# Attention of 160 tiles: TensorE's order per tile becomes scores, values of the tile two back, turning of the tile one back

## The reference

```python
s = jnp.einsum('bqhd,bqkhd->bhqk', qb, kg) * ATTN_SCALE
s = jnp.where(valid[:, None], s, -jnp.inf)
p = jax.nn.softmax(s, axis=-1)
o = jnp.einsum('bhqk,bqkhd->bqhd', p, vg)
```

```python
def gqa_attention(q, k, v):
    ...
        logits = jnp.einsum("bqhgd,bkhd->bhgqk", qb, k).astype(jnp.float32) * scale
        p = jax.nn.softmax(logits, axis=-1).astype(v.dtype)
        return jnp.einsum("bhgqk,bkhd->bqhgd", p, v)
```

## Time and profile before

| | |
|---|---|
| median of 3 runs | 3273.68 us (3270.32 to 3275.79) |
| span of the profiled execution, its only time | 3279.7 us |
| TensorE busy | 3142.8 us (96%) |
| VectorE, ScalarE, GpSimd busy | 47%, 40%, 34% |
| scores L1347, 2064 matmuls | 213.3 us |
| turning L1805, 1312 | 182.9 us |
| values L1820, 2624 | 178.6 us |

### The profile page before, as it was taken

The page is one execution under the profiler, slowest core; times in us unless marked ns, Lnnn a source line. Parts: engine busy times, 40 slices in busy tenths (PEclk is TensorE's granted clock), DMA queues, the critical chain, the costliest instruction groups (busy, mean ns, idle before and its releaser), DMA issues. The chain is left out here.

```text
span 3279.7 us, 50609 instructions
## 1 busy us (share of the span) xinstructions
PE 3142.8 (96%) x20584; PEld 2584.5 (79%) x20584; DVE 1545.7 (47%) x2748; ACT 1307.4 (40%) x2383; POOL 1121.1 (34%) x613
## 2 busy tenths in 40 slices
PE   9989999999989999999999999999999998799999
PEld 7757788888667888888887888887888877688787
DVE  5963343227853344242376410268333349843473
ACT  4352333223433333233466222267222248723463
POOL 4531444446324444434201222243224422125202
PEclk9998999999999999999999999999999999999999
DMA  4344222324452223222000112110112200013102
GB/s 163 114 171 171 84 97 97 100 88 134 144 199 90 96 97 111 97 84 82 27 2 21 58 58 65 54 48 15 53 64 87 87 20 1 12 53 111 39 2 78
DMA packets 80806, 259.92 MB, mean 79 GB/s; under 512 B 11968, under 2 KB 13376, under 8 KB 80576
## 3 DMA queue, kind: packets, MB, share of 16 engines
q1 hardware_dynamic: 80576, 256.69, 23.6%
HBM read 239.34 MB, written 2.10 MB: 74 GB/s over the span
## 5 line engine op out<-in xcount | busy, mean ns | idle before, releaser
L188 PE MATMUL ps<-hs,head 128*128 128x512 f32 (+1 forms) x4176 | 864.1, 364 | 18.8 <-DVE hs L1068 8.6
L188 PE MATMUL ps<-hs,WS 128*128 128x512 f32 (+1 forms) x4176 | 858.3, 363 | 6.0 <-POOL WS L169 5.9
L188 PEld LDWEIGHTS ps<-hs,head 128*128 128x128 f32 x4176 | 711.2, 189 | 160.4 <-issue 13.4
L188 PEld LDWEIGHTS ps<-hs,WS 128*128 128x128 f32 x4176 | 713.0, 189 | 134.4 <-POOL WS L169 8.3
L169 POOL TENSOR_TENSOR WS<-W,WS 128x1024 fp32r<-128x1024 f32 x168 | 407.0, 2423 | 645.2 <-ACT WS L161 645.2
L169 POOL TENSOR_TENSOR head<-W,head 128x1024 fp32r<-128x1024 f32 x165 | 400.6, 2428 | 624.6 <-ACT head L161 624.6
L161 ACT CAST WS<-W 128x1024 fp32r<-128x1024 f32 x168 | 176.1, 1048 | 339.7 <-PE ps L188 314.1
L1838 ACT ACTIVATE prob<-ps,low 128x768 f32<-128x768 f32 (+4 forms) x320 | 223.4, 700 | 180.1 <-DVE low L1910 177.7
L1910 DVE TENSOR_REDUCE low<-ps 128x1 f32<-128x768 f32 (+4 forms) x320 | 216.6, 702 | 93.5 <-PE ps L1347 89.1
L161 ACT CAST head<-W 128x1024 fp32r<-128x1024 f32 x165 | 172.7, 1047 | 199.4 <-PE ps L188 196.0
L1347 PE MATMUL ps<-kk,qq 64*128 64x256 f32 (+3 forms) x2064 | 213.3, 333 | 24.8 <-ACT prob L1574 14.7
(11 more groups left out here) (323 smaller groups left out, 3756.9 us busy)
## 6 DMA issues: line engine op xcount, KB each, us to landing
W<-in_stream_dram SPq DMA_DIRECT2D x433, 512.0 KB, 3.3
swap<-prj SPq DMA_DIRECT2D x168, 64.0 KB, 2.5
band<-in_bias_band_dram SPq DMA_DIRECT2D x8, 512.0 KB, 3.6
prj<-prj SPq DMA_DIRECT2D x64, 64.0 KB, 2.8
xT<-in_x_dram SPq DMA_DIRECT2D x4, 512.0 KB, 6.3
out_dram<-xT SPq DMA_DIRECT2D x8, 256.0 KB, 2.7
W<-in_stream_dram SPq DMA_DIRECT2D x1, 1536.0 KB, 10.8
xT<-in_ctx_dram SPq DMA_DIRECT2D x1, 1024.0 KB, 7.4
```

What stands on the lines that cost most here:

```text
L188: last = pe.matmul(out, a(i), b(j), start=start and n == 0, stop=stop and n == 2)
```

## The change

On TensorE, the block that turns tile x-1 is moved behind the block that multiplies the values of tile x-2. The waits of both blocks go with them, and their contents stay as they are. The side work's mix stays ahead of both, its products behind both. No other engine's program is changed.

```diff
@@ -1793,18 +1793,6 @@
                             keep_running(pe, M, 4, 7)
                     if side:
                         side.mix(pe, x)
-                    if 1 <= x <= X:
-                        y = x - 1
-                        for hd in range(2):
-                            pe.wait_ge(exped, 2 * y + hd + 1)
-                            if y:
-                                pe.wait_ge(turn_copied, act_copies(y - 1) + 1 if hd == 0 else act_copies(y))
-                                if dve_copies(y) and (hd or W.tail(y)):
-                                    pe.wait_ge(dve_turn_copied, dve_copies(y))
-                            for j, sc in enumerate(W.columns(y)):
-                                last = pe.transpose(turn_at(y, hd, j), prob[:, (2 * y + hd) % 4, sc:sc + P],
-                                                    M.const[:, C_ID:C_ID + P])
-                            last.then_inc(turned, 1)
                     if x >= 2:
                         y = x - 2
                         p, nb = works[y][1], len(W.blocks(y))
@@ -1825,6 +1813,18 @@
                                              inv[:, 2 * y + hd:2 * y + hd + 1].broadcast_to([P, 64]),
                                              M.const[:, C_ID:C_ID + P], start=True, stop=True)
                         last.then_inc(weighted, 1)
+                    if 1 <= x <= X:
+                        y = x - 1
+                        for hd in range(2):
+                            pe.wait_ge(exped, 2 * y + hd + 1)
+                            if y:
+                                pe.wait_ge(turn_copied, act_copies(y - 1) + 1 if hd == 0 else act_copies(y))
+                                if dve_copies(y) and (hd or W.tail(y)):
+                                    pe.wait_ge(dve_turn_copied, dve_copies(y))
+                            for j, sc in enumerate(W.columns(y)):
+                                last = pe.transpose(turn_at(y, hd, j), prob[:, (2 * y + hd) % 4, sc:sc + P],
+                                                    M.const[:, C_ID:C_ID + P])
+                            last.then_inc(turned, 1)
                     if side:
                         side.products(pe, x)
```

## The result

The changed kernel takes 3336.47 us (median of four runs, 3328.64 to 3340.51) against 3274.55 for the kernel before in the same runs (3270.32 to 3275.79): a ratio of 1.0189, 95% interval 1.0176 to 1.0201. It is 61.9 us slower; the forecast was 3320, with a range of 3295 to 3350. The direction and the places were right, the size came out 16 us short.

The account below looks back on a forecast made before the run. TensorE, busy 96% of the span, was taken as the bound; the terms 16.1 + 9.0 + 5.6 + 11.5 + 4.5 = +46.7 us gave 3320.4 against the median 3273.7, forecast as 3320, range 3295 to 3350.

Parts of the forecast that it names:

- The two loops: Loops through VectorE (768-key tiles 4.65 us, small tiles 2.55) and ScalarE (512-key neighbourhood tiles 3.73) set the periods.
- the terms: Steady-state losses: shared-key tiles +16.1 us, small context tiles +9.0 and +5.6, neighbourhood tiles +11.5.
- its own case: Both loops cost what was summed, whole kernel: 3320 us, own range 3309 to 3332, chance 53%.
- the terms' bounds: Low and high limits of all stages' losses, adding up to +27 and +76 us, so 3301 to 3350.
- That turning no longer waits: Rival: values fill turning's 14.7 us of waits for exponentials and nothing else waits, 3259 us; chance 6%.
- That nothing moves: Rival: the loops come out equal to the periods before, in all tiles, 3274 us; chance 5%.
- only ScalarE's loop and the small tiles: Rival: in 768-key tiles the scores cover the hand-overs, so 16 us fall away, 3304 us; chance 17%.
- The delayed gate also delays the maximum: Rival: 0.17 us more per loop in every tile outside the first block, +21 us, 3341 us; chance 15%.
- this term: First block: about one tile in four waits for a late gate or copy, +4.5 us (0 to 9).
- the estimate: First block, values of tile 5: a wait of 1.0 us for the gate behind VectorE's query split.
- The clock stays 1.00: Sign expected in the changed profile: TensorE's granted clock remains full, 2.4 GHz.
- that rival: The clock falls on the 30 small context tiles, at most +44 us, 3364 us; chance 4%.

Follow-up runs that it names:

- The early gate: The changed kernel with VectorE's gate of tile x-2 done ahead of its copy of turned tile x-1: 3300.17 us, ratio 1.0085.
- the kernel with one product: The changed kernel with one unread product of constants between scores and values of each small context tile outside the first block: 3340.16 us, ratio 1.0206.
- the two kernels with the gate early: The changed kernel with VectorE's gate ahead of its copy, 3300.17 us; the same with both ScalarE copies between the exponentials, 3279.39 us.

## Why the prediction was right, and where it was short

**The two loops** were right, to the hand-over. Periods forecast and measured: 4.65 and 4.67, 2.55 and 2.59, 3.73 and 3.73. Each loop was then opened alone, by an edit on the engine that it runs over and with TensorE's order unchanged, and each time the period of its own tiles fell back while the other kept its value. By the periods the steady part is 0.28 x 62 = 17.4, 0.64 x 15 = 9.6, 0.37 x 31 = 11.5, and 6.4 behind the neighbourhood layer: 44.9 where the terms say 42.2. The measured 3336 is above the 3309 to 3332 that the forecast gave to its own case; that it lies in the range of 3295 to 3350 is owed to the width of the terms' bounds, and most of the 15 us between 47 and 62 are the two things below.

**The rivals.** That turning no longer waits decided nothing: that wait fell by 9 us, but the values took over a larger one. That nothing moves, or only ScalarE's loop and the small tiles, is ruled out by 4.67. "The delayed gate also delays the maximum" gives a time near the one measured (3341) for a reason that is not there: it wanted 0.17 more in every loop outside the first block, and the loops were 0.00 to 0.04 over. The maximum does start later (L1910 at 1659.25 above, behind both gates), and its tile is scored 4.67 apart all the same.

**First block: this term was too small**, +10.6 in the profiles and +13 (9 to 18) by the run of that part alone, for +4.5. The profiles' figure is rough: in those with the old order of the first block and the late gate, one layer took anything from 61.0 to 65.4 us. The step itself is there. Timeline of step 7, as in the earlier trace rows:

```profile
195.20 0.40 DVE L1926 COPY probT<-ps 128x256 f32<-128x256 f32 x1
...
195.52 0.68 DVE L1315 SCALAR_TENSOR_TENSOR qq<-prj,qq 128x512 fp32r<-128x512 f32 x1
...
196.44 0.29 DVE L1894 TENSOR_TENSOR hT<-hT,ps 128x128 f32<-128x128 f32 x1
...
196.98 1.02 PE L1128 MATMUL ps<-const,row 128*128 128x2 f32 x8 [0.97 <-DVE hT L1894]
```

TensorE stands 0.97 us for the gate behind the query split; 1.0 was the estimate. What I had missed is that the split isn't always 0.68 long, that the clock can fall behind such a wait, and that one such step can then be worth far more. Timeline of step 11 of the same layer:

```profile
210.89 2.37 POOL L1158 TENSOR_TENSOR w<-w,prj 128x1024 f32<-128x1024 f32 x1
...
211.57 2.25 DVE L1315 SCALAR_TENSOR_TENSOR qq<-prj,qq 128x512 fp32r<-128x512 f32 x1
...
214.05 0.29 DVE L1894 TENSOR_TENSOR hT<-hT,ps 128x128 f32<-128x128 f32 x1
...
214.59 1.02 PE L1128 MATMUL ps<-const,row 128*128 128x2 f32 x8 [2.08 <-DVE hT L1894]
...
217.33 1.94 PE L1113 MATMUL ps<-W,cond 128*32 128x512 f32 x8
```

The split takes 2.25 us here, the gate behind it ends at 214.34, and TensorE stands 2.08 us. Behind that its granted clock falls. Window of the changed kernel, with busy times by engine, then granted clock, DMA share and GB/s:

```profile
217.00:221.00 4.00, 4.00 (x33) 1.90 (x30) 1.34 (x7) 2.25 (x6) 0.97 (x1) 0.58 0.22 52
```

At 0.58, near the lower of the two levels (1.2 GHz), eight ada products take 1.94 us instead of 1.06 (before) and the next scores 0.90 instead of 0.55. From the scores of tile 11 to those of tile 12 it is 7.66 us where it was 4.28. The step ahead of it is 1.08 shorter than before, so the two together grow by 2.3.

The second layer has no slow split (0.72). Its large step is 7: TensorE stands the same 0.97 us for the gate, and there the clock falls behind it. Window of the changed kernel:

```profile
897.00:901.00 4.00, 4.00 (x30) 2.31 (x28) 1.38 (x5) 2.13 (x7) 3.70 (x5) 0.68 0.22 84
```

That step takes 7.00 us instead of 4.69; the first layer's step 7, at a granted clock of 1.00, takes 5.50. So part of the first block's loss is the clock behind the new waits, which the prediction counted nowhere. In the two layers together the steps with a split (2, 7, and 10 with 11) hold 6.8 us of the growth.

The slow split isn't a thing of the new order alone. Timeline of step 11 of the first layer in the kernel with only the shared-key layers changed, whose first block has the old order:

```profile
211.00 2.37 POOL L1158 TENSOR_TENSOR w<-w,prj 128x1024 f32<-128x1024 f32 x1
211.09 2.83 DVE L1315 SCALAR_TENSOR_TENSOR qq<-prj,qq 128x512 fp32r<-128x512 f32 x1
...
214.70 1.02 PE L1128 MATMUL ps<-const,row 128*128 128x2 f32 x8 [2.32 <-DVE hT L1907]
```

TensorE stands 2.32 us, and the step takes 7.37. With the late gate the split of this group took over 2 us in 7 of 10 layers profiled with the new order and in 2 of 8 with the old; whether the order brings that about or chance does isn't shown. The early gate helps only in part: the same split is just as slow (2.20) and its step takes 4.75, but the masks and maxima of tile 11 stand behind it as well, ScalarE's copy for the values of tile 10 comes after them, and TensorE stands 1.81 us one step later (4.40 for 2.53). The two layers take 65.8 and 66.4 us in that kernel.

**What no term counted: the ends of the stages.** Of the 62.1 us some 7 are left when the periods' 44.9 and the first block's 10.6 are taken off. They lie where the loop is run out: the last two passes have no scores that would cover a hand-over. From the last scores to the last values the neighbourhood layer takes 8.2 us instead of 4.9, the first shared-key layer 7.1 instead of 4.9, the last layer 12.0 instead of 10.0. Timeline of the last values behind the neighbourhood layer:

```profile
2337.38 0.66 PE L1808 MATMUL ps<-probT,vtok 128*64 128x128 f32 x8 [0.58 <-DVE prj L1894]
...
2339.97 1.12 PE L1808 MATMUL ps<-probT,vtok 128*64 128x128 f32 x8 [1.13 <-DVE prj L1894]
```

The wait doubles from 0.58 to 1.13, and the values take 1.12 instead of 0.66, at a lower clock; the last block, at 2343.69, has the same two numbers. In the kernel with one product, whose clock is full up to the end of both stages, the two waits are the same (1.12 to 1.13), the values take 0.66, and the run-out is 6.8 us in both layers. So 1.9 us of it are the loop, and in the changed kernel the lower clock adds 0.3 and 1.4.

**The clock.** "The clock stays 1.00" was wrong at the edges. Windows of the changed kernel: context tiles behind the shared-key layer, the 20 us behind these, and the context tiles of the neighbourhood layer:

```profile
1765.00:1807.00 42.00, 30.86 (x331) 23.05 (x332) 24.90 (x91) 22.10 (x78) 4.35 (x6) 0.97 0.01 2
1807.00:1827.00 20.00, 20.00 (x103) 17.23 (x104) 10.64 (x11) 9.97 (x13) 5.04 (x2) 0.90 0.24 78
2303.00:2346.00 43.00, 31.93 (x331) 23.79 (x330) 25.14 (x94) 23.74 (x85) 8.45 (x12) 0.93 0.01 2
```

Before, the corresponding windows show 1.00. In the changed kernel the clock is 1.00 up to 1799 and 2339, and 0.87 and 0.57 in the 7 us from there, where the stages end. In the kernels with the 2.59 period and no filling, the clock fell in or just behind such a stage in four visits of six. In the two kernels with the gate early, at 2.03, it fell in none of four; but where the context tiles had the old order and the old gate, it was 0.91 in the 20 us behind them in three visits of eight, so the gaps alone don't decide it. The Trainium skill, "TensorE: Matmul & The Clock Gate" (Part 1, the HAM clock gate), says that the clock is halved when the engine isn't busy enough. This trace agrees in part: the fall stands where TensorE's waits are longest (1.13 us), but with the same waits the kernel with one product kept 1.00. Over most of the stage, where TensorE stands 0.57 us of each 2.59, the clock is full, so the 44 us of that rival didn't come, and the filled kernel shows how little hangs on it. The kernel with one product, window of the first context tiles:

```profile
1770.00:1809.00 39.00, 37.30 (x357) 25.93 (x355) 24.03 (x88) 22.31 (x79) 4.36 (x6) 1.00 0.01 2
```

1.00 in the stage (0.91 in the 20 us behind it), and no time gained that the runs can tell, though the two stages are 0.3 and 1.4 us shorter. What the lower clock behind the stages costs was not measured by itself.

## What to carry to other kernels

When a step of one engine is moved behind another, sum the closed loop that this makes through the other engines, pitch by pitch and for each kind of tile, and compare it with the period; here that held to 0.04 us. Then walk the in-order queue that carries the loop in its irregular steps and in the last passes: a side operation that is harmless in the old order (a split of 0.68 us) makes the bound engine stand 0.97 us in the new one, and one of over 2 us costs in either order (2.08 and 2.32 us of waiting). The orders of the engines belong together: the same move of a gate was worth 34 us one way with one order of TensorE and 30 us the other way with the other.

## What the runs showed of the hardware that was not expected

**A VectorE operation three times its length beside GpSimd.** The query split (two inputs in SBUF, 128x512) has a median of 0.69 us over ten. In the kernel before it began at 210.93, ahead of GpSimd's multiply L1158 at 211.27, and took 0.81, and GpSimd's took 2.71. In the changed kernel GpSimd's began first, at 210.89 for 2.37 us, and the split, begun at 211.57, took 2.25: it ends 0.56 after GpSimd's does, by these rows. Each first-block layer has one such split beside GpSimd's multiplies (L1157, then L1158), 24 in the twelve profiles. In every one the split ends 0.55 us after the end of the GpSimd multiply that was running when it began. It took over 2 us in the 15 where L1158 had begun 0.08 to 0.84 us ahead of it, and 0.70 to 0.81 in the nine where the running multiply was near its end. This says that the split waits for GpSimd's operation, as far as timing can say it (spans on GpSimd are rough); no run took that operation away. The Trainium skill, "GPSIMD Engine Reference" (section 1, Specifications), says that GpSimd shares its SBUF interfaces with VectorE and that they contend when VectorE's instruction has two SBUF inputs, as this one has; the rows agree.

**Filling with short products.** Two constant products of 256 columns in fp32, which the trace shows as four records, cost 1.06 us of TensorE's time, and one, two records, stayed within a gap of 0.57.
